# Gate weights split before u, head maxima stacked on 36 rows, and identity turns moved beside two weight streams

## The reference

```python
for l in range(DEPTH):                                   # first_block, DEPTH = 2
    ada = (c_act @ w_ada[l] + b_ada[l])[:, None, :]
    sh1, sc1, g1, sh2, sc2, g2 = jnp.split(ada, 6, axis=-1)
    u = h * (1.0 + sc1) + sh1
    y = mixer(u, w_in[l], ...)                           # mLSTM branch, dilated attention, output gates
    h = layer_norm(DN_ALPHA * h + g1 * y, ln1_g[l], ln1_b[l])
    u = h * (1.0 + sc2) + sh2
    y = swiglu(u, w1[l], w3[l], w2[l])                   # (silu(u @ w1) * (u @ w3)) @ w2
    h = layer_norm(DN_ALPHA * h + g2 * y, ln2_g[l], ln2_b[l])
```

## Time and profile before

| | |
|---|---|
| runs | 1978.60, 1984.53, 1991.67 us |
| profiled execution, device time | 1995.85 us |
| its span (first to last instruction) | 1994.0 us |
| mean granted clock of PE | 0.989 |
| busy PE, DVE, ACT | 1928.2 (97%), 1417.4 (71%), 1039.5 (52%) us |
| chain that ended last | PE 80%, DVE 12%, ACT 4%, issue 2%, DMA 2% |
| mean DMA rate | 180 GB/s |

### The profile page before, as it was taken

How to read it: one execution, slowest core, us unless ns; L and a number is a source line. 1 busy time by engine, 2 the same in 40 slices (tenths; PEclk the granted TensorE clock), 3 DMA queues, 4 the chain that set the end, 5 groups by cost and what they waited for, 6 DMA issues and landing times.

```text
span 1994.0 us, 37262 instructions
## 1 busy us (share of the span) xinstructions
PE 1928.2 (97%) x15718; PEld 1841.0 (92%) x15718; DVE 1417.4 (71%) x2559; ACT 1039.5 (52%) x1597; POOL 22.2 (1%) x36
## 2 busy tenths in 40 slices
PE   5999999999999999999999999999999999999998
PEld 5999999999999999999999988879999988799998
DVE  7777686687668876776675558986766589967565
ACT  3564465454446644664544435565655445665554
POOL 1100000000002000000000000000000000000000
PEclk8999999999999999999999999999999999999999
DMA  8555555548763564545475525432655343325552
GB/s 324 177 188 193 213 184 183 187 183 302 260 224 130 190 222 166 199 174 192 168 253 191 197 103 188 145 106 85 219 188 181 139 148 128 123 90 190 190 187 89
DMA packets 52770, 358.98 MB, mean 180 GB/s; under 512 B 5995, under 2 KB 8651, under 8 KB 9980
## 3 DMA queue, kind: packets, MB, share of 16 engines
q1 hardware_dynamic: 52476, 356.54, 50.0%
q10 hardware_dynamic: 128, 0.07, 0.0%
HBM read 355.41 MB, written 1.08 MB: 179 GB/s over the span
## 4 chain that ended last, share of the span: by engine, by line
PE 80%; DVE 12%; ACT 4%; issue 2%; DMA 2%; SPq 0%; ACTq 0%; DVEq 0%
PE projected L476 34%; PE projected L1513 18%; PE mixed L476 8%; PE mixed L1513 6%; PE projected L1531 2%; DVE W L2118 2%; DVE w_lo L393 2%; DVE w_lo L1455 1%; PE mixed L634 1%; PE projected L1567 1%; DMA w_mod<-in_first_ada_dram 1%; PE mixed L1665 1%; PE mixed L1638 1%; PE mixed L542 1%; PE mixed L555 1%
## 5 line engine op out<-in xcount | busy, mean ns | idle before, releaser
L393 DVE TENSOR_TENSOR w_lo<-raw,w_hi 128x1024 fp32r<-128x1024 f32 x340 | 409.4, 1226 | 224.5 <-ACT w_hi L739 223.4
L739 ACT ACTIVATE w_hi<-raw 128x1024 fp32r<-128x1024 f32 x338 | 349.8, 1057 | 304.7 <-PE projected L476 256.5
L476 PE MATMUL projected<-u_hi,w_hi 128*128 128x256 f32 x1728 | 486.9, 282 | 5.8 <-DVE u_lo L949 3.1
L476 PE MATMUL projected<-u_lo,w_hi 128*128 128x256 f32 x1728 | 480.9, 278 | 0.0
L476 PE MATMUL projected<-u_hi,w_lo 128*128 128x256 f32 x1728 | 480.8, 278 | 0.0
L476 PEld LDWEIGHTS projected<-u_hi,w_hi 128*128 128x128 f32 x1728 | 325.8, 189 | 11.4 <-issue 10.0
L476 PEld LDWEIGHTS projected<-u_hi,w_lo 128*128 128x128 f32 x1728 | 325.7, 188 | 0.0
L476 PEld LDWEIGHTS projected<-u_lo,w_hi 128*128 128x128 f32 x1728 | 324.8, 188 | 0.0
L1455 DVE TENSOR_TENSOR w_lo<-raw,w_hi 128x1024 fp32r<-128x1024 f32 x200 | 240.9, 1222 | 111.5 <-ACT w_hi L1809 111.5
L1809 ACT ACTIVATE w_hi<-raw 128x1024 fp32r<-128x1024 f32 x200 | 207.0, 1055 | 134.1 <-PE projected L1513 106.6
L1513 PE MATMUL projected<-u_hi,w_hi 128*128 128x256 f32 x960 | 270.9, 282 | 0.8 <-DVE w_lo L1455 0.8
(11 more groups left out here) (381 smaller groups left out, 3870.3 us busy)
## 6 DMA issues: line engine op xcount, KB each, us to landing
raw<-in_stream_dram SPq DMA_DIRECT2D x324, 1024.0 KB, 4.9
w_mod<-in_first_ada_dram SPq DMA_DIRECT2D x8, 1024.0 KB, 14.9
band<-bias_rows SPq DMA_DIRECT2D x1, 3072.0 KB, 13.1
x<-in_xT_dram SPq DMA_DIRECT2D x1, 1024.0 KB, 4.9
out_dram<-uf SPq DMA_DIRECT2D x4, 256.0 KB, 2.5
tri<-in_tri_dram SPq DMA_DIRECT2D x2, 384.0 KB, 4.4
c<-in_c_dram SPq DMA_DIRECT2D x1, 512.0 KB, 6.6
mask<-in_mask_dram SPq DMA_DIRECT2D x1, 384.0 KB, 25.5
```

Source lines behind the costliest of these rows:

```text
L393: eng.tensor_tensor(part(w_lo, step, half), raw_half(step, half), part(w_hi, step, half).bitcast(F32), ALU.subtract).then_inc(s_lo_dve, 1)
L476: m = pe.matmul(out, a, b, start=start and n == 0, stop=stop and n == 2, **kw)
L739: act.activation(part(w_hi, step, half), raw_half(step, half), ACT.Copy).then_inc(s_hi, 1)
```

## The change

**Gate weights.** `wgate_hi` and `wgate_lo` of layer 0 are made in the prologue (ACT behind `rstd`, DVE in the middle of its `w_mod` products), those of layer 1 in the last norm of layer 0 (`ln`, i = 1), on ACT behind the squares, on DVE behind the `fold` operations. In step `u` they are gone.

**Maxima.** A tensor `peaks` of 36 rows takes the four rows of maxima: rows 0 to 3 the rounded part (ACT, at the end of `qk_silu` 6), rows 32 to 35 the rest (DVE, in `qk_silu` 7), zeros between (DVE memset in `gate_rows`). `sel_m` holds the matching selector, made once by two small ACT copies. One product of 512 columns takes the place of the two plain float32 products of a head. PE's `ml_scores` waits for `peaks` and `sel_m` too.

**Identity turns.** The four transposes ahead of the first `w2` of each layer stand behind the wait for its `w_lo` now, next to the product. In block 2, four transposes are added ahead of `wg` 1 of each layer.

```diff
+    sel_m = nc.alloc_sbuf_tensor_at("sel_m", [STACK, MH], F32R, offset=k["ones1_at"] + 320)
...
+    peaks = nc.alloc_sbuf_tensor_at("peaks", [STACK, 2, T], F32R, offset=area + 98 * KB + 512)
...
             elif kind == "ml_scores":
                 pe.wait_ge(s_qk, 8 * l + 8)
                 pe.wait_ge(s_rows, 2 * l + 2)
+                pe.wait_ge(s_pkl, l + 1)
                 if i == 0:
+                    pe.wait_ge(s_sel, 2)
...
-                for d in range(2):
-                    m = pe.matmul(MB[1][:, d * T:(d + 1) * T], ident[0:MH, i:i + 1].to_broadcast([MH, P]),
-                                  rows[:, d, 0, :], start=True, stop=True)
-                m.then_inc(s_msc, 1)
+                pe.matmul(MB[1][:], sel_m[:, i:i + 1].to_broadcast([STACK, P]), peaks[:, :, :],
+                          start=True, stop=True).then_inc(s_msc, 1)
...
             elif kind == "w2":
                 pe.wait_ge(s_hid, N + 1)
-                if i == 0:
-                    turn_idle(pe, MB[3], ident, 4)
...
                 for kt in range(2) if i < FP - 1 else ():
                     hi, lo = split(step, kt)
+                    if i == 0 and kt == 0:
+                        turn_idle(pe, MB[3], ident, 4)
...
+                if N == 0:
+                    act.activation(sel_m[0:32, :], ident[0:32, 0:MH], ACT.Copy).then_inc(s_sel, 1)
+                    act.activation(sel_m[32:STACK, :], ident[32:STACK, 32:STACK], ACT.Copy).then_inc(s_sel, 1)
                 if i == 0:
-                    act.activation(wgate_hi[:], wgate[:, l], ACT.Copy).then_inc(s_gw_hi, 1)
...
                 act.activation(qkT[:, 2 * i:2 * i + 2, :], sth[i % 2][:], ACT.Silu).then_inc(s_qk, 1)
+                if i == 6:
+                    act.wait_ge(s_rows, 2 * l + 2)
+                    act.wait_ge(s_pk0, l + 1)
+                    act.activation(peaks[0:MH, :, :], rows[:, :, 0, :], ACT.Copy).then_inc(s_pkh, 1)
...
+                if i == 1 and l + 1 < DEPTH:
+                    act.wait_ge(s_gt, l + 1)
+                    act.activation(wgate_hi[:], wgate[:, l + 1], ACT.Copy).then_inc(s_gw_hi, 1)
...
-                if i == 0:
-                    dve.wait_ge(s_gw_hi, l + 1)
-                    dve.tensor_tensor(wgate_lo[:], wgate[:, l], wgate_hi[:].bitcast(F32), ALU.subtract).then_inc(s_gw_lo, 1)
...
+                dve.wait_ge(s_pkh, l + 1)
+                dve.tensor_tensor(peaks[32:STACK, :, :], rows[:, :, 0, :], peaks[0:MH, :, :].bitcast(F32),
+                                  ALU.subtract).then_inc(s_pkl, 1)
...
             elif kind == "gate_rows":
+                dve.memset(peaks[:, :, :].bitcast(F32), 0.0).then_inc(s_pk0, 1)
                 dve.wait_ge(s_gd, 64 * l + 64)
...
+                if i == 1 and l + 1 < DEPTH:
+                    dve.wait_ge(s_gw_hi, l + 2)
+                    dve.tensor_tensor(wgate_lo[:], wgate[:, l + 1], wgate_hi[:].bitcast(F32), ALU.subtract)\
+                       .then_inc(s_gw_lo, 1)
...
             elif kind == "wu" or kind == "wg" and i:
+                if kind == "wg" and i == 1:
+                    turn_idle(pe, bank(step), ident, 4)
                 project(step, (u_hi, u_lo))
...
         act.activation(rstd[:], lnv[:], ACT.Exp, scale=-0.5).then_inc(s_rstd, 1)
+        act.wait_ge(k["sems"]["s_small"], 32)
+        act.activation(wgate_hi[:], wgate[:, 0], ACT.Copy).then_inc(k["sems"]["s_gw_hi"], 1)
...
         for i in range(KT):
+            if i == KT // 2:
+                dve.wait_ge(k["sems"]["s_gw_hi"], 1)
+                dve.tensor_tensor(wgate_lo[:], wgate[:, 0], wgate_hi[:].bitcast(F32), ALU.subtract)\
+                   .then_inc(k["sems"]["s_gw_lo"], 1)
```

More of the change, by code:

```diff
@@ L42 @@
 MH, MD = 4, 256
+STACK = 32 + MH
 TAPS1 = 5
@@ L303, in first_block @@
     s_rows = sem("gate_rows_ready")
+    s_pk0 = sem("peak_rows_cleared")
+    s_pkh = sem("peak_rows_rounded")
+    s_pkl = sem("peak_rows_rest_ready")
+    s_sel = sem("head_selector_ready")
     s_gct = sem("gate_columns_turned")
@@ L441, in first_block @@
              modulations=(s_ada, len(ADAS)), products=(s_used, 2 * len(MAIN1)), last_var=(s_var, 2 * DEPTH),
-             s_scaled=s_scaled, rstd1=rstd, turned=(s_hm, MH * DEPTH))
+             wgates=(wgate, wgate_hi, wgate_lo), s_scaled=s_scaled, rstd1=rstd, turned=(s_hm, MH * DEPTH))
     def sync(sp):
@@ L2287, in prologue @@
     psum = k["PB"]
+    wgate, wgate_hi, wgate_lo = k["wgates"]
     k.update(s_rowc=s_rowc, s_rowd=s_rowd, bias_row=bias_row)
```

## The result

Over 22 executions of each kernel on one chip, the changed kernel takes 1976.51 us (median, 1963.49 to 1983.61), the kernel before 1987.41 us (1978.60 to 1999.33). The ratio is 0.9946, 95% interval 0.9931 to 0.9961: 0.5% or 10.8 us faster. That lies inside the predicted range, 8.5 us above the predicted 1968. The same two kernels in a later session gave 0.9983 (0.9964 to 1.0002), 3.9 us by the medians. The two intervals do not meet, so the size of the gain is less sure than either of them says.

A forecast was written before the change was run, and what follows sets the result against it. PE's work was taken as the bound (busy 97%). From the profiled execution, 1995.85 - 5.3 - 6.3 - 5.3 - 12.3 = 1966.7 us; from the fastest run 1968.8. It took 1968, range 1962 to 1980.

The forecast's parts named there:

- Gate weights: Gate products, both layers: early `wgate_hi` and `wgate_lo` remove PE's waits and layer 0's clock drop, 5.3 us, at least 3.8.
- the clock's part: Layer 0 gate products: without the 2.46 us wait PE's clock stays at full speed, 1.54 us more.
- DVE did not take the gain back: Rival, `qk` stage: DVE sets the pace, the earlier start is lost in `gate_rows`; costs 4 of 5.3 us, 1972; chance 0.07.
- Maxima: Heads: one product for spreading saves 0.72 us each, 5.8 for eight; less 0.5 memset, plus 1.0 faster streams: 6.3 us.
- The 1.0 us for faster streams: Heads: some 450 products behind the new spreading product mostly run at the fast rate; 1 us, bounds 0 to 2.
- Turns in block 1: First `w2` streams: layer 1 turns fast, 6.2 us, layer 0 stays fast, transposes cost 0.9; net 5.3, bounds -7.1 and 5.3.
- Turns in block 2: Ahead of `wg` 1: 1476 products behind turn fast, 6.6 us each layer, 13.2, less 0.9 for transposes; net 12.3.
- the turns don't fix the rate, and only cost: Rival, feed-forward streams: fast or slow as before, turns cost 1.8 us; 1974.7; chance 0.30, shared with block 2 slow (1981).
- The turns fix the slow rate: Rival: all four feed-forward streams turn slow, as at `v` 0; 1992.2 us, 0.4% slower than the median; chance 0.06.
- whole steps of 6.5 us apart: Runs of before differ by slow feed-forward stages: three cost 19.4 us, the median holds about one, the profiled execution three.
- The clock: Rival: idle time or turns lower PE's clock at five places, 1.7 us each, 8.4 in all; 1976; chance 0.05.

The follow-up runs named there:

- the maxima alone: The kernel before with only the maxima stacked on 36 rows (`sel_m`, `peaks` and what fills them): ratio 0.9990 (0.9974 to 1.0006).
- three transposes alone: The kernel before with three identity transposes added ahead of `wg` 1 of each layer of block 2: ratio 0.9999, median 1979.42 us.
- the turns alone: The kernel before with only the two edits on the identity turns, in block 1 and block 2: ratio 0.9981, median 1985.61 us.
- 20 turns a layer: The changed kernel with four transposes ahead of every `wg` and `wu` chunk of block 2 with i over 0: profiled span 1991.3 us.
- The kernel whose streams are set at a place that worked each time: The changed kernel with three transposes ahead of `wg` 2 and 3 instead of four ahead of `wg` 1: 1969.94 us, ratio 0.9912.

## Why the prediction held, and where its reasons failed

**Gate weights: right.** Predicted 5.3 us: the wait and the fallen clock of layer 0 (4.0) and the wait of layer 1 (1.3). `v` 0 starts 4.25 us earlier in layer 0, the clock stays up, both sets of 24 products take 2.8 us, and the freed span gives 6.4. That number has the clock's part taken out, so it stands against 3.8, a little over the 2 us of doubt that it has; for both parts together it is 9.9 against 3.8 and the 4.6 below, 8.4; the eight freed spans give 8.5.

The clock's part is not sure in each execution: four profiled executions have the long wait for `wgate_lo`, and behind it a stretch at 0.50 follows in three (before, the maxima alone, three transposes alone), but not in that of the turns alone, whose chain has the gate products at full speed behind a wait of 2.50 us:

```profile
47.23 2.99 PE mixed L476 x24
```

In the ten without the wait it never does. So the edit saves the 1.54 us only in an execution in which the clock would have fallen. DVE did not take the gain back: behind the wait in `gate_rows` the 120.38 of before had become 116.32, 4.06 us earlier, which is the 4.25 less the 0.18 of the memset. That rival is out.

**Maxima: right in mechanism, a little high.** Predicted 6.3 us. The price of the new product was set at 0.33 us from `decay`; it is 0.43 on the chain, so a head gains 0.63 and not 0.72: 5.0 and not 5.8. The memset costs 0.18 us a layer, 0.36 and not 0.5. The 1.0 us for faster streams behind it did not come: from the first score product to the last head's turn 427 of 1040 split products were slow against 477, 0.2 us, but over all profiles the mean is 461 in the ten kernels or repeats with the new form and 458 in the four with the old. Sum 5.0 - 0.4 = 4.6; freed span 5.4.

**Turns in block 1: the gain was not there to be had.** The step "layer 1's stream is slow, the turn makes it fast, 6.2 us" took the profiled execution for the rule. In the four other profiled kernels that still have the turn ahead of the wait, both streams are fast: with before that makes 9 of 10 streams. Directly behind the turn it is 18 of 18. So a turn may help there, and what it can help is one stream in ten, 2 x 0.1 x 6.2 = 1.2 us, for 0.9 us of transposes.

**Turns in block 2: the step that failed.** It said that a stream behind transposes runs fast, by eight fast places in block 1, and priced 12.3 us. Those places were no law for others. The eight fast ones and the slow `v` 0 had one thing in common that I passed over: each place had its own outcome. Over the 14 profiled executions `wa` was fast 28 times in 28, the chunk behind the running `ml_turn` of the first three heads 84 in 84 (24 from slow, 60 from fast), and `v` 0 slow 27 in 28. The turn at `wg` 1 exchanged the rates in all 8 streams that met it as the first thing behind `wu` 0 (the changed kernel twice, the turns alone, and 20 turns a layer): six from slow to fast, two from fast to slow. Over the 14 profiled executions `wu` 0 was slow 17 times in 28. Without a turn that leaves (17/28) x 2 x 6.6 = 8.0 us of slow stages in a mean execution, with an exchange (11/28) x 2 x 6.6 = 5.2: a gain of 2.8 us, less 0.9 for the transposes, in place of 12.3. The placement was also read from a pair like `ml_turn`, "a slow chunk, four transposes, a fast one". That was true there, and there four transposes, of the head's output instead of the identity, also leave a fast stream fast. Before, layer 0, chain:

```profile
204.88 5.65 PE projected L476 x48
210.53 0.44 PE projected L644 x4
210.97 5.46 PE projected L476 x48
```

(The first chunk's 5.65 us include its start behind the maxima; its products lie 113 ns apart, so it is a fast one.) What failed was to carry the outcome of that place over to `wg` 1, where a turn exchanges.

**The sum came out inside the range by way of a rival.** Nearest to what happened is the first one, "the turns don't fix the rate, and only cost" (they do move the rate, by exchange, but gain little by it): from before's median less the gate weights and the maxima plus 1.8 us, 1974.7 us by the three runs shown, 1977.6 from the median of 22. Measured: 1976.5. It had a chance of 0.30, the forecast 0.52. The range reached up to 1980 for its sake, and that is why it held. Counted from the profiled execution, 17.6 of the forecast's 29.2 us were the turns', and those were not there to be had in a mean execution. The evidence against the forecast stood in the text: `v` 0 in both layers. One counter-example against eight was weighed as one in nine, when a mechanism that has a counter-example at a like place has to explain it first. "The turns fix the slow rate" in all streams was out as well.

**The profile as a measure.** The argument that the runs of before are whole steps of 6.5 us apart was right in kind: freed of the three slow stages before's execution would take 1995.85 - 19.4 = 1976.4 us, and its fastest executions in the sessions took 1970.9 to 1980.4. But it then took the fastest of three runs as "nearly all fast" and the median as one slow stage. By 22 runs the median lies about 11 us above 1976.4, nearer to two. And 1970.9 lies 5.5 us below the 1976.4, so more varies between executions than these stages.

**The clock** moved as little as forecast, but it moves by itself: 30.7 us at half clock in the first profile of the changed kernel, 40.9 in the second, 37.5 in that of before. Part of what the first profile gained (6.8 us of half clock, 3.7 us) was such luck.

What stays open: which property of the engine holds a rate and why transposes exchange it at one place and not at another. No run here shows that. Nor is it shown that the executions without a profile lose their time to slow streams, since their traces don't exist. The kernel whose streams are set at a place that worked each time spreads over 7 us and the changed kernel over 20, but the first has six executions and the second 22, and the maxima alone, whose streams nothing sets, spread over 8 us in 12.

## What to carry to other kernels

Two profiles of single executions can differ by three times what the kernels differ by; count what is drawn anew in each execution (a rate, a clock stretch), take it out of both spans, and compare the rest with the terms of the sum. Where an operation is said to have a side effect on the engine behind it, put it at twenty places of one kernel and read the outcomes in both directions: one profiled run of that kind told exchange from cure at one kind of place from the other, where the medians of four kernels could not. An interval of half a per cent can't confirm a term of 5 us; a span freed of luck nearly can.

## What the runs showed of the hardware

- A stream of split products (256 columns, at the granted clock 1.00) has two steady rates, 113.3 and 117.8 ns from start to start, and keeps the one it starts with for 1380 or 1476 products. The Trainium skill (page "TensorE: Matmul & The Clock Gate", section "Back-to-back issue gap") gives 109 ns by its warm formula, which it calls the gap of an isolated product, and for streams it has figures for 128 and 512 columns alone; no stream here ran at 109, and the measured rates decide. Transposes of 128 columns lie 108 to 109 ns apart.
- In block 2's feed-forward stage four identity transposes in a running stream exchange the two rates behind a projection chunk (43 times in 49) and keep them behind a `wd` chunk (18 in 18). Two exchange them (5 in 5). Three end fast 28 times in 29, 14 of 15 from slow and 14 of 14 from fast. One has no rule that I could read. Plain products of the identity, 2 to 8 records, left a fast stream fast 20 times in 20; a slow one was not tried. In block 1 the four transposes of a head's `ml_turn` in a running stream, also between projection chunks, ended fast 84 times in 84, so the kind of chunk ahead doesn't decide alone. Those transposes turn a head's output and not the identity; which difference counts is not shown.
- A spreading of 512 columns from 36 rows costs 0.43 us on the chain, start to start 0.42, where two of 48 rows in a row had shown 0.33 each.
- The same kernel had three stretches of 3.4 us at half clock beside the opening one in one profiled execution and six in another, 1.8 us each; over all 14 profiles there were three to seven.
